# One ring buffer of a 1 MB gather ring given up for a head's weights

## The reference

```python
def one_chunk(xc):                                   # per token
    q = (xc @ w_q).reshape(CHUNK, HEADS, 2, D_HALF)  # 8 heads, 2 x 128
    s = einsum('thcd,hcnd->thcn', q, subkeys)        # 128 keys a side
    s_top, i_top = top_k(s, 16)
    ... best 16 of the 16 x 16 sums -> idx, g = softmax(best)
    u = u_tab[idx]; v = v_tab[idx]                   # 16384 rows of 1024 each
    act = gelu(einsum('td,thkd->thk', xc, u))
    return einsum('thk,thkd->td', g * act, v)
```

## Time and profile before

| | |
|---|---|
| runs | 1514.26 us median of 3 (1512.84 to 1515.54) |
| profiled execution | 1513.23 us, span 1511.4 us |
| busy | DVE 1088.9, PE 1038.8, ACT 615.2, POOL 580.1 us |
| DMA | 603.29 MB, of which the gathers 536.90 MB |
| slots | the first gather is issued at 105.8 us, the last at 1488.6 us |

### The profile page before, as it was taken

One profiled execution on the slowest core, in us unless ns is written; L12 is line 12 of the kernel. 1 busy time (PEld: TensorE's weight loads), 2 busy tenths in 40 slices (PEclk: granted clock), 3 DMA queues, 4 the chain that ended last, 5 costly groups with the idle time before them and its releaser, 6 DMA issues.

```text
span 1511.4 us, 20941 instructions
## 1 busy us (share of the span) xinstructions
PE 1038.8 (69%) x6816; PEld 515.5 (34%) x6816; DVE 1088.9 (72%) x2934; ACT 615.2 (41%) x1856; POOL 580.1 (38%) x516
## 2 busy tenths in 40 slices
PE   9999876777756777666778777665777554444543
PEld 5645432322433454332334455332244211010100
DVE  5448668777645799998746788698786676666784
ACT  2324555553423446554244535354344433233321
POOL 0013444443333454543433434344334444444441
PEclk9999986567777788787887788578888755555555
DMA  9639999999999999999999999999999999999996
GB/s 388 242 137 398 419 419 419 418 413 413 416 420 419 420 397 419 418 415 397 418 420 420 402 417 414 420 415 397 412 407 417 417 419 420 419 420 419 420 418 268
DMA packets 82649, 603.29 MB, mean 399 GB/s; under 512 B 9734, under 2 KB 10502, under 8 KB 12012
## 3 DMA queue, kind: packets, MB, share of 16 engines
q0 software_dynamic: 73728, 536.90, 86.3%
q1 hardware_dynamic: 7852, 64.74, 10.5%
q10 hardware_dynamic: 960, 0.31, 0.1%
HBM read 600.87 MB, written 1.05 MB: 398 GB/s over the span
## 4 chain that ended last, share of the span: by engine, by line
DMA 39%; PE 21%; DVE 20%; issue 13%; ACT 6%; POOL 1%; SPq 0%; DVEq 0%; POOLq 0%; ACTq 0%
DMA ring<-table_dram,idx 37%; PE bank L637 8%; DVE ring L1695 8%; PE ypsum L637 6%; PE qpsum L637 4%; ACT L1104 2%; DVE arena L1578 2%; PE spsum L637 1%; POOL ring L630 1%; DMA arena<-c_out_dram 1%; ACT wts L1104 1%; DVE topi L1627 1%; ACT gel L1104 1%; DMA ring<-w_in_dram 1%; DVE eq L1628 1%
## 5 line engine op out<-in xcount | busy, mean ns | idle before, releaser
L630 POOL DMA_INDIRECT ring<-table_dram,idx x512 | 579.9, 1133 | 909.2 <-PE ypsum L637 540.4
L1695 DVE CUSTOM_DVE_ANT_0 ring<-xns,ring 128x1024 f32<-128x1024 f32 x512 | 623.3, 1223 | 295.5 <-DMA ring<-table_dram,idx 292.3
L637 PE MATMUL ypsum<-ring,wts 128*32 128x256 f32 x4096 | 425.3, 504 | 428.5 <-ACT wts L1104 427.7
L1104 ACT ACTIVATE gel<-dot 128x1 f32<-128x1 f32 x512 | 103.2, 202 | 714.9 <-DVE dot L1695 713.4
L637 PEld LDWEIGHTS ypsum<-ring,wts 128*32 128x32 f32 x4096 | 96.0, 124 | 681.5 <-ACT wts L1104 624.3
L1104 ACT ACTIVATE wts<-gident,gel 128x32 f32<-128x32 f32 x512 | 164.6, 321 | 17.4
L1104 ACT ACT_TABLE_LOAD x83 | 106.5, 1283 | 5.2 <-issue 3.8
L637 PE MATMUL qpsum<-arena,hT 128*128 128x256 f32 (+1 forms) x416 | 99.5, 414 | 2.4 <-ACT hT L1104 2.4
L1578 DVE SCALAR_TENSOR_TENSOR arena<-arena,cols 128x128 f32<-128x128 f32 x300 | 88.5, 346 | 0.6
L637 PE MATMUL qpsum<-arena 128*128 128x128 f32 x372 | 83.7, 361 | 0.0
L637 PEld LDWEIGHTS qpsum<-arena,hT 128*128 128x128 f32 (+1 forms) x416 | 71.9, 193 | 26.1 <-issue 12.9
(11 more groups left out here) (194 smaller groups left out, 1018.3 us busy)
## 6 DMA issues: line engine op xcount, KB each, us to landing
arena<-heads_dram SPq DMA_DIRECT2D x12, 1152.0 KB, 9.8
head<-heads_dram SPq DMA_DIRECT2D x8, 1152.0 KB, 10.1
ring<-table_dram,idx POOLq DMA_INDIRECT x512, 13.2
arena<-c_in_dram SPq DMA_DIRECT2D x4, 2048.0 KB, 19.1
ring<-w_in_dram SPq DMA_DIRECT2D x3, 2048.0 KB, 18.1
arena<-c_out_dram SPq DMA_DIRECT2D x6, 1024.0 KB, 9.0
arena<-w_out_dram SPq DMA_DIRECT2D x1, 4096.0 KB, 37.2
arena<-heads_dram SPq DMA_DIRECT2D x1, 3456.0 KB, 16.4
```

The costliest lines, as they stand in the source:

```text
L630: pool.indirect_dma_start(out=row(b), out_offset=None, in_=table[:, :], in_offset=bass.IndirectOffsetOnAxis(ap=idx[R % 2][:, k:k + 1], axi ...
L637: return nc.tensor.matmul(o_, l, r, start=start, stop=stop, **kw)
L1104: return nc.scalar.activation(out_, in_, func, **kw)
L1695: V.tensor_tensor_reduce(out=u, in0=xnr[G % 2], in1=u, scale=1.0, scalar=0.0, op0=ALU.mult, op1=ALU.add, accum_out=dot[:, k:k + 1]).then_i ...
```

## The change

- `RING` is 6: gather n waits for the matmuls of slot n - 6. The freed space, with what `rep` gives back, becomes a room for one head, `ring_room`.
- Chunk 0 of the projection weights now lies on the score space and `ring_room`. The second tile's chunks are multiplied in the order 2, 0, 1, 3.
- Phase 0's head 4 is fetched whole into `ring_room`, when chunk 0 has been multiplied, instead of in three parts during the attention. It stays for phase 1: seven stay, one is fetched again.
- Layer 1 streams through four rooms, three stay for phase 3, five are fetched again (two DMAs instead of three).
- `rep` is one matrix, which ACT rewrites after each group's rows were taken out; PE waits for it (`rep_ready`).

```diff
-RING = 7
+RING = 6
-            [NORM_AT[0] + N_NORM + 3, NORM_AT[0] + N_NORM + 1, NORM_AT[0] + N_NORM, NORM_AT[0] + N_NORM + 2, SECOND + 6]]
+            [NORM_AT[0] + N_NORM + 1, NORM_AT[0] + N_NORM + 2, NORM_AT[0] + N_NORM, NORM_AT[0] + N_NORM + 3, SECOND + 6]]
-HEAD_ORDER = [(4, 5, 6, 7, 0, 1, 2, 3), (2, 5, 3, 1, 4, 7, 6, 0), (0, 1, 2, 3, 4, 5, 6, 7), (7, 5, 0, 1, 2, 3, 4, 6)]
-AGAIN = (HEADS + 4, HEADS + 5)
+HEAD_ORDER = [(4, 5, 6, 7, 0, 1, 2, 3), (2, 5, 3, 1, 7, 6, 0, 4), (0, 1, 2, 3, 4, 5, 6, 7), (5, 6, 7, 0, 1, 2, 3, 4)]
+AGAIN = HEADS + 4
-KEPT = HEADS - 2
+KEPT = HEADS - 3
+STREAMS = 4
...
-        rep = sb("rep", GROUPS * P)
+        rep = sb("rep", P)
...
-        ring = sb("ring", RING * 2 * D + ROUNDS * 2 * KEYS)
+        ring = sb("ring", RING * 2 * D + ROUNDS * 2 * KEYS + HEAD_W)
+        ring_room = ring[:, RING * 2 * D + ROUNDS * 2 * KEYS:RING * 2 * D + ROUNDS * 2 * KEYS + HEAD_W]
...
-        first_room = [None, proj_room[0], head, tile_room, head2, uq_room, ukv_room, proj_room[1]]
-        next_room = [ukv_room, proj_room[0], proj_room[1], uq_room, again_room[0], again_room[1], head, head2]
-        stream = [acc_room, head, head2]
-        last_room = [head, head2] + [kept[:, i * HEAD_W:(i + 1) * HEAD_W] for i in range(KEPT)]
+        first_room = [ring_room, proj_room[0], head, tile_room, head2, uq_room, ukv_room, proj_room[1]]
+        next_room = [ukv_room, proj_room[0], proj_room[1], uq_room, again_room, head, head2, ring_room]
+        stream = [acc_room, head, head2, ring_room]
+        last_room = [head, head2, ring_room] + [kept[:, i * HEAD_W:(i + 1) * HEAD_W] for i in range(KEPT)]
... (SP)
-            full(sp, HEAD_AT[0] + 3 * (HEADS - 1))
-            load_part(half_w[1], head_no(0), half, HEAD_K, first_in[0])
...
-            load_part(half_w[0], head_no(0), 0, half, first_in[0])
-            full(sp, OUT_AT + KD - 1)
-            load_part(split_keys, head_no(0), HEAD_K, HEAD_W, first_in[0])
             full(sp, EARLY_S)
             load_first(1)
             load_first(2)
+            full(sp, PROJ_JOB[1][0])
+            load_first(0)
...
-                    for a, b in ((0, 3), (3, 5), (6, 7)):
+                    for a, b in ((0, 3), (3, KEPT)):
...
-                    load_again(0)
-                    load_again(1)
+                    load_head(again_room, 0, head_no(AGAIN), again_in)
... (PE)
-                    mm(bank[:, :], rep[:, g * P:(g + 1) * P], xn[:, half * CHUNK:(half + 1) * CHUNK], True, True)\
+                    if G and half == 0:
+                        pe.wait_ge(rep_ready, G)
+                    mm(bank[:, :], rep[:, :], xn[:, half * CHUNK:(half + 1) * CHUNK], True, True)\
...
+            project(1, 0)
             project(1, 1)
             project(1, 3)
-            project(1, 0)
... (ACT)
+                if halves[-1] == 1 and G + 1 < PHASES * GROUPS:
+                    g = (G + 1) % GROUPS
+                    run(rep[:, :].rearrange("p (s t) -> p s t", s=QUAD),
+                        ident[:, g * QT:(g + 1) * QT].unsqueeze(1).to_broadcast([P, QUAD, QT])).then_inc(rep_ready, 1)
```

More of the change, by code:

```diff
@@ L207, in stream_room @@
 def stream_room(H):
-    return (H - STREAM) % 3
+    return (H - STREAM) % STREAMS
 def stream_turn(H):
-    return (H - STREAM) // 3 + 1
+    return (H - STREAM) // STREAMS + 1
 def head_slot(p, h):
@@ L358, in build @@
         acc_room = arena[:, at_acc:at_acc + HEAD_W]
-        again_room = [arena[:, conv_size["cin"] + i * HEAD_W:conv_size["cin"] + (i + 1) * HEAD_W] for i in range(2)]
+        again_room = arena[:, conv_size["cin"]:conv_size["cin"] + HEAD_W]
         early_room = [head2, head, proj_room[1], proj_room[0]]
         early_scores = gident[:, 2 * KEYS:4 * KEYS]
-        half_w, split_keys = [part["pp"], part["qT"]], o[:, D - 2 * KEYS:D]
-        first_room = [None, proj_room[0], head, tile_room, head2, uq_room, ukv_room, proj_room[1]]
-        next_room = [ukv_room, proj_room[0], proj_room[1], uq_room, again_room[0], again_room[1], head, head2]
-        stream = [acc_room, head, head2]
-        last_room = [head, head2] + [kept[:, i * HEAD_W:(i + 1) * HEAD_W] for i in range(KEPT)]
-        first_parts = [3, 1, 1, 2, 0, 1, 1, 1]
+        first_room = [ring_room, proj_room[0], head, tile_room, head2, uq_room, ukv_room, proj_room[1]]
+        next_room = [ukv_room, proj_room[0], proj_room[1], uq_room, again_room, head, head2, ring_room]
+        stream = [acc_room, head, head2, ring_room]
+        last_room = [head, head2, ring_room] + [kept[:, i * HEAD_W:(i + 1) * HEAD_W] for i in range(KEPT)]
+        first_parts = [1, 1, 1, 2, 0, 1, 1, 1]
         quad_room = [early_room, first_room[0:QUAD]]
         def weights_in(room, k):
-            if room is None:
-                return half_w[k // (KD // 2)][:, k % (KD // 2) * 2 * HALF:(k % (KD // 2) + 1) * 2 * HALF]
             return room[:, k * 2 * HALF:(k + 1) * 2 * HALF]
         def keys_in_room(room, c):
-            if room is None:
-                return split_keys[:, c * KEYS:(c + 1) * KEYS]
             return room[:, HEAD_K + c * KEYS:HEAD_K + (c + 1) * KEYS]
@@ L391, in room_of @@
             return stream[stream_room(H)] if streamed(H) else last_room[h]
-        quarter_gain, same_row, last_rows = xns[:, 0:DQ], rep[:, 0:P], hT[:, 0:DQ]
+        quarter_gain, same_row, last_rows = xns[:, 0:DQ], rep[:, :], hT[:, 0:DQ]
         squares, square_sum = hT[:, DQ:2 * DQ], hT[:, 2 * DQ:2 * DQ + 1]
@@ L415, in build @@
         uq_in, ukv_in, wout_in = sem("uq_in"), sem("ukv_in"), sem("wout_in")
-        again_in = [sem(f"again_in{i}") for i in range(2)]
-        stream_in = [sem(f"stream_in{i}") for i in range(3)]
+        again_in = sem("again_in")
+        stream_in = [sem(f"stream_in{i}") for i in range(STREAMS)]
         kept_in = sem("kept_in")
+        rep_ready = sem("rep_ready")
         gain_in = sem("gain_in")
@@ L591, in _ @@
                     load_cin(2)
-                    full(sp, s_job(HEADS + 5))
+                    full(sp, s_job(AGAIN))
                     load_conv_out(0)
-                    for H in (STREAM + 1, STREAM + 2):
-                        full(sp, s_job(H - 3))
+                    for H in range(STREAM + 1, STREAM + STREAMS):
+                        full(sp, s_job(H - STREAMS))
                         load_stream(H)
@@ L602, in _ @@
                     load_stream(STREAM)
-                    for H in range(STREAM + 3, LAST_PHASE):
-                        full(sp, s_job(H - 3))
+                    for H in range(STREAM + STREAMS, LAST_PHASE):
+                        full(sp, s_job(H - STREAMS))
                         load_stream(H)
@@ L1234, in beside_attention @@
                 if s == 7:
-                    full(act, q_job(0))
                     latents(1)
@@ L1382, in _ @@
             replicate(0)
-            project(1, 1)
+            project(1, 0)
             peer_exp(0)
             first_use(ACT.Gelu)
-            project(1, 3)
+            project(1, 1)
             for n in range(ALL_SLOTS):
@@ L1730, in beside_attention @@
                 if s == 10:
-                    full(dve, s_job(0))
                     rotate_key(1)
@@ L1803, in _ @@
             V.tensor_copy(ident16[:, :], ident[:, :]).then_inc(id_ready, 1)
-            own.did(V.tensor_copy(rep[:, :].rearrange("p (g s t) -> p g s t", g=GROUPS, s=QUAD),
-                                  ident[:, :].rearrange("p (g t) -> p g t", g=GROUPS).unsqueeze(2).to_broadcast([P, GROUPS, QUAD, QT])))
+            own.did(V.tensor_copy(rep[:, :].rearrange("p (s t) -> p s t", s=QUAD),
+                                  ident[:, 0:QT].unsqueeze(1).to_broadcast([P, QUAD, QT])))
             own.then(V.tensor_copy(posf[:, :], posi[:, :]))
```

18 lines of the change are left out of this document (6 added, 12 removed).

## The result

The changed kernel takes 1542.4 us (median of 6 runs, 1536.25 to 1545.85) against 1514.22 us (6 runs, 1512.84 to 1515.54) for the kernel before on the same chip: ratio 1.0183, interval 1.0172 to 1.0195, so 28 us slower. The prediction was 1519 with a range up to 1530. The sign was right; the time lies outside the range, and the loss is six times the +4.7 of the sum.

A forecast was written before the change was run, and what follows sets the result against it. The prediction took DMA bytes, plus any time the DMA engines stand idle, as the bound. It summed -5.6 (loads), +5.0 (start) and +5.3 (ring) to +4.7 us, giving 1519 us, range 1509 to 1530.

The forecast's parts named there:

- The loads: Phases 1 and 3: two head loads of 1152 KB fall away where the queue is full, -5.6 us.
- The spreading matrix: ACT rewrites `rep` 15 times, 0.39 us each, where the reserve is large: 0 us.
- The start: First gathers: the new chunk order issues four of them later, 5.0 us of DMA time lost.
- One buffer less: All 505 reissued gathers: each leaves when the next one left before; idle DMA time sums to 5.3 us.
- issue + 3.3 - landing of gather n - 1: At each reissue: engine idle time, where positive, using the next gather's old issue time; eight single places, 4.3 us.
- the lead of 3.3: Every gather: 3.3 us needed beside its 2.5 us transfer, from one issued onto an empty queue and used 5.8 later.
- The holes at output products: Attention's and both tiles' convolution output products: loads issued there fill most of the holes, leaving 0.7 and 0.3 us.
- the single places: Eight places where DVE routes or taps or PE has a long block: 0.3 to 0.8 us idle each, 4.3 in all.
- The subtraction itself: Over the reissues: release of slot n - 6 is what gather n + 1 waited for, so POOL's rows give new issue times.
- Slower by much: Rival: the lead is nearer 4.2, so the ring costs about 20 us; about 1533, over +12 us, chance 0.15.
- No change: Rival: lead about 2.5, ring costs 0 to 1 and start 3 to 5; near 1513.5, chance 0.23.
- faster: Rival: start and ring together cost 0 to 2, so the two loads win; 1509 to 1511 us, chance 0.22.

The follow-up runs named there:

- ring of six: The kernel before with six gather buffers instead of seven and nothing else changed: 1547.14 us, ratio 1.0217.
- six in slots 20-255: The kernel before, seven buffers kept; gathers of slots 20 to 255 wait for one slot more, as if six: 1528.74 us, ratio 1.0105.
- six in slots 256-399: The kernel before, seven buffers kept; gathers of slots 256 to 399 wait for one slot more, as if six: 1526.07 us, ratio 1.0083.
- late by two: The kernel before; 14 gathers of the last phase wait for two more slots than their buffer needs: 1522.42 us, ratio 1.0056.
- late by three: The kernel before; 14 gathers of the last phase wait for three more slots than their buffer needs: 1535.23 us, ratio 1.0137.
- late by four: The kernel before; 14 gathers of the last phase wait for four more slots than their buffer needs: 1563.99 us, ratio 1.0327.

## Why the prediction was wrong

**The loads**: -5.6 said, -6.3 measured. Right. **The spreading matrix**: 0 and 0. Right. **The start**: +5.0 said, +3.8 alone and +3.9 at slot 7 of the kernel after. Right in size, with two details wrong. Head 4's load did not wait for its hole but slowed the second gather by 1.9 us. And gather number 6 of the kernel before, issued at 121.62, was not in at 127.4 but at 129.4, by its last landing (15 of its 16 are in the trace). Number 5 had landed at 124.8, so number 6 had a reserve of 3.2 us and landed 4.6 behind it, 2.1 more than a transfer. By the last landing that is a lead of 5.3, in a row of the kernel before.

**One buffer less**: +5.3 said, about +29 measured (the two stretches; 33 with what the ring of six loses at the start, and 31 as what is left of the 28.2 when -6.3 and +3.9 are taken off). This is the term that failed, and within it the step "issue + 3.3 - landing of gather n - 1": the lead of 3.3 was set against the last landing of the gather ahead. The prediction took 3.3 us from a gather that found the queue empty, "as these places are like the first gather: a queue found empty", and kept 5.1, from the second gather of the same rows, as an upper bound alone. Counted over slots 20 to 399 by reserve: number of gathers, and in brackets the us by which their landings together exceeded steps of 2.5 (the bytes of loads that fall there are in it):

```
reserve, us            under 3      3 to 5       5 to 6
before                  0            4 (11.4)    18 (7.6)
six in slots 20-255     8 (24.4)    17 (16.3)    36 (1.8)
six in slots 256-399    9 (26.8)    18  (9.0)    31 (6.5)
ring of six            13 (35.2)    34 (25.5)    42 (3.4)
after                  15 (33.4)    34 (15.7)    40 (5.8)
```

In the last two rows the 68 gathers with a reserve of 3 to 5 us exceed by 0.6 on the mean, the 82 with 5 to 6 by 0.1, and 206 with 6 to 8 by 0.15. So the loss begins at about 5, where the prediction's lead let all of the middle column but its lower end go free, and that column went from 4 gathers to 34. But 5.1 is not the lead that should have stood in the sum either: 29 of the 68 landed within 2.6 us of their forerunners, and with 5.1 the shortfalls over slots 20 to 399 come to twice the loss or more (third column below).

What fits is the distance between the 16 landings of one gather: at the median the first comes 3.1 us ahead of the last in the kernel before, and 2.2 in the ring of six. Where nothing more is queued, an engine that is done early waits while the last still moves data. Number 6 above shows it: its first landing was at 126.7, 5.1 after its issue, just as that of the gather onto the empty queue, their mean at 127.8, close to the 127.4 of the prediction, and the last at 129.4. Counted in each trace after the fact, with the prediction's own 3.3, once against the last landing and once against each of the 16 with the mean taken over them; all in us, less the same count for the kernel before:

```
slots 20 to 399         measured   last, 3.3   last, 5.1   each of 16, 3.3
ring of six               32.6       22.5        70.8        34.8
six in slots 20-255       14.3       12.8        42.5        15.3
six in slots 256-399      15.5       12.6        42.3        14.7
after                     26.0       19.4        69.7        29.5
slots 390 to 511
late by two                6.6        2.4        12.6         8.2
late by three             19.8        4.6        24.5        17.6
late by four              47.5       32.6        67.5        48.5
```

The measured column is the difference of the landings; to the 20.4 of after are added the 5.6 of the two loads that it leaves out. The last column is within 3.5 us in all seven, and its 3.3 was not fitted (with 3.0 it is within 5.2). So the size of the lead was about right; what was wrong is that the reserve was counted from the last landing, as if all 16 engines ran dry together. No run changed the distance between the engines by itself, so this is an agreement of seven counts and not an experiment.

The Trainium skill (DMA: Bandwidth & Descriptors, Anatomy of one DMA) gives such a gather about 2.0 us beside its bytes. No run here supports a lead that small: the gather onto an empty queue needed 3.1 to 3.3 beside its transfer, and the least from issue to last landing is 5.3 in the trace after and 5.6 in the one before, 2.8 and 3.1 beside it.

**The holes at output products.** The prediction let the loads issued there fill them: 0.7, 0.15 and 0.15 us. In the kernel after, POOL and SP in the first tile's convolution product:

```profile
721.57 0.94 POOL L618 DMA_INDIRECT ring<-table_dram,idx  x1 [0.30 <-issue]
729.74 0.94 POOL L618 DMA_INDIRECT ring<-table_dram,idx  x1 [7.23 <-PE ypsum L625]
735.31 1.07 POOL L618 DMA_INDIRECT ring<-table_dram,idx  x1 [4.63 <-PE ypsum L625]
```

```profile
728.36 0.35 SPq L534 DMA_DIRECT2D arena<-c_out_dram  x1
...
733.61 0.35 SPq L537 DMA_DIRECT2D arena<-c_out_dram  x1
```

```profile
722.96 5.37 PE L625 MATMUL bank<-arena,hT 128*128 128x512 f32 x8 [3.18 <-issue]
728.26 0.64 PE L625 MATMUL ypsum<-ring,wts 128*32 128x256 f32 x8
```

The load goes out at 728.36, 1.6 us before the last gather of the queue has landed (730.0), and the next gather at 729.74. The next three landings are at 736.5, 742.4 and 745.0: 15.0 us, less 7.5 for the gathers and 5.0 for the two loads, is 2.5 lost. The load waits for the same block of PE as the gather (PE's product runs to 728.3), so it is late itself. The other two products lose 2.6 (attention's, slots 95 to 98) and 3.0 (slots 346 to 350), as the difference of the same steps in the two traces: 8.1 us instead of 1.0. The remaining 21 or so of the 29 are the single places, said to be 4.3. Against the last landing and with 3.3 the measured reserves give 7 for them, against each of the 16 landings 20 to 24.

**What stays open.** The subtraction itself, the issue time of the next gather for that of this one, did well: it puts 21 gathers of slots 20 to 399 under a reserve of 3.3, and the ring of six has 18. Single places are off either way: 1.2 measured where it says 2.8 at slot 159, 2.0 for 3.8 at slot 175, 4.3 for 3.4 at slot 270. How the loss is to be forecast from the rows of before alone stays open. The count against each of the 16 landings, done over those rows with the delays carried on, gives 60 us, since it keeps the engines 3.1 us apart where the ring of six has them at 2.2. Why they are apart no run shows.

**The rivals.** "Slower by much" came nearest, +19 at a lead of 4.2, with the 5.1 and the uneven restart of the engines among its reasons. Its lead for all places is not what the traces show, so its nearness is in part luck. "No change" and "faster" needed a lead of 2.5 or a hidden start; neither was seen. The waits of the kernel after have no new row of PE for `heads_dram` or `rep`. One mark of the prediction was blunt: it named slices of DMA under nine tenths in the middle as the sign of being wrong, and there were none. The one that spoke was its sign of being right, 418 to 420 GB/s in the steady stretches: they had 412 and 394.

No version made here beats the kernel before; the one that ran faster leaves loads out.

## What to carry to other kernels

A landing as the profile gives it is the last of 16, and the engines that were done earlier are dry before it. So a queue's reserve is shorter than the last landing says, for the first engine here by 2 to 3 us; where two rows of one trace give different leads (3.3 and 5.1 here), the places that the larger one adds should be counted first, and a third row looked for. One buffer of a ring is worth what it does to the requests at the short end: here 4 gathers under 5 us of reserve became 49, while the median gather still went out 10.8 us ahead of its landing. A transfer fills a hole only if it does not wait for the same block that makes the hole.

## What was not expected of the hardware

- A gather of 1.05 MB onto an empty queue is used 5.8 us after its issue, 3.3 beside its transfer. In a running queue the loss begins when less than about 5 us of transfers, by the last landing, are ahead of a gather: 0.6 us on the mean for the 68 with 3 to 5, though 29 of them followed within 2.6 us.
- The 16 landings of one gather are 3.1 us apart at the median in the kernel before and 2.2 with six buffers. In one place of the kernel after the shortfall appears twice: steps of 4.0 and 4.2 us for two gathers in a row, issued with 1.8 and 3.6 us of reserve.
- The rate falls before the busy share does: 419 to 410 GB/s at a DMA share of 1.01.
